# Expert weights in one table per token block, and 24 blocks' outputs for the first token block inside the rounds of inputs

## The reference, cut to what matters

```python
q = (xt @ wq).reshape(PEER_BLOCK, PEER_HEADS, PEER_KEY_DIM)
s1 = jnp.einsum('thd,nd->thn', q[..., :PEER_HALF], subkeys1)
s2 = jnp.einsum('thd,nd->thn', q[..., PEER_HALF:], subkeys2)
v1, i1 = lax.top_k(s1, PEER_TOPK)
v2, i2 = lax.top_k(s2, PEER_TOPK)
cand = (v1[..., :, None] + v2[..., None, :])          # 16 x 16 candidates
vals, pos = lax.top_k(cand, PEER_TOPK)
ids = e1 * PEER_N_KEYS + e2                           # one of 16384 experts
g = jax.nn.softmax(vals, axis=-1)
a = jnp.einsum('td,thkd->thk', xt, u_tab[ids])
hid = jax.nn.gelu(a) * g
y = jnp.einsum('thk,thkd->td', hid, v_tab[ids])
x = layer_norm(DN_ALPHA * x + y, ln2_g, ln2_b)
```

## Time and profile before

| | us |
|---|---|
| three runs, median | 1095.2 |
| lowest and highest | 1092.23, 1096.01 |
| the profiled execution | 1094.1 |
| its span in the trace | 1092.1 |
| PE busy | 1019.6 (93%) |
| DVE busy | 837.4 (77%) |
| POOL busy | 453.3 (42%) |
| ACT busy | 450.8 (41%) |

### The profile page before, as it was taken

How to read it: one execution, slowest core, us unless ns; L and a number is a source line. 1 busy time by engine, 2 the same in 40 slices (tenths; PEclk the granted TensorE clock), 3 DMA queues, 4 the chain that set the end, 5 groups by cost and what they waited for, 6 DMA issues and landing times.

```text
span 1092.1 us, 20382 instructions
## 1 busy us (share of the span) xinstructions
PE 1019.6 (93%) x6766; PEld 935.8 (86%) x6766; DVE 837.4 (77%) x1484; ACT 450.8 (41%) x648; POOL 453.3 (42%) x332
## 2 busy tenths in 40 slices
PE   7999999899999999999999999129999999999995
PEld 6878897899999999999999999128888888888884
DVE  3475457677999998988888888028888888888887
ACT  3474444344443334444444444004444444444442
POOL 5800000058888888888888888840000000000000
PEclk9999999899999999999999999659999999999998
DMA  9676688545665566877777775247777777777773
GB/s 310 233 270 222 208 289 299 177 117 113 140 135 138 146 139 150 199 172 169 159 176 170 173 167 103 0 120 239 238 240 241 241 241 240 240 242 240 243 239 126
DMA packets 146735, 210.41 MB, mean 193 GB/s; under 512 B 47376, under 2 KB 95312, under 8 KB 146704
## 3 DMA queue, kind: packets, MB, share of 16 engines
q1 hardware_dynamic: 109264, 208.58, 58.5%
q0 software_dynamic: 37440, 1.43, 9.9%
HBM read 192.00 MB, written 17.96 MB: 192 GB/s over the span
## 4 chain that ended last, share of the span: by engine, by line
PE 49%; POOL 38%; issue 8%; DVE 3%; ACT 1%; DMA 1%; POOLq 0%; DVEq 0%; SPq 0%; ACTq 0%
POOL expert_weights L457 38%; PE ps L1274 32%; PE ps L1192 14%; PE ps L1088 1%; ACT w_hi L575 1%; DVE w_lo L902 1%; PE ps L1066 1%; DMA xres<-in_x_dram 1%; DVE xres L701 0%; DVE xres L708 0%; PE ps L1038 0%; PE ps L1076 0%; DMA expert_weights<-gw,cell 0%; DVE small L689 0%; DVE v_lo L982 0%
## 5 line engine op out<-in xcount | busy, mean ns | idle before, releaser
L457 POOL DMA_INDIRECT expert_weights<-gw,cell x256 | 413.5, 1615 | 258.9 <-DVE gw L895 178.7
L1232 PE MATMUL ps<-act_hi,uT_hi 128*128 128x256 f32 x1024 | 295.1, 288 | 0.0
L1232 PE MATMUL ps<-act_hi,uT_lo 128*128 128x256 f32 x1024 | 289.9, 283 | 0.0
L1232 PE MATMUL ps<-act_lo,uT_hi 128*128 128x256 f32 x1024 | 289.7, 283 | 0.0
L655 ACT ACTIVATE v_hi<-v_raw 128x512 fp32r<-128x512 f32 x256 | 147.9, 626 | 245.1 <-PE ps L1274 198.3
L1274 PE MATMUL ps<-v_hi,hid_hi 128*128 128x512 f32 x512 | 158.4, 391 | 45.0 <-DVE v_lo L982 45.0
L1232 PEld LDWEIGHTS ps<-act_lo,uT_hi 128*128 128x128 f32 x1024 | 196.6, 192 | 0.0
L1232 PEld LDWEIGHTS ps<-act_hi,uT_hi 128*128 128x128 f32 x1024 | 196.6, 192 | 0.0
L1232 PEld LDWEIGHTS ps<-act_hi,uT_lo 128*128 128x128 f32 x1024 | 196.3, 192 | 0.0
L982 DVE TENSOR_TENSOR v_lo<-v_raw,v_hi 128x512 fp32r<-128x512 f32 x256 | 164.9, 686 | 0.0
L1274 PE MATMUL ps<-v_lo,hid_hi 128*128 128x512 f32 x512 | 158.1, 390 | 0.0
(11 more groups left out here) (149 smaller groups left out, 1392.2 us busy)
## 6 DMA issues: line engine op xcount, KB each, us to landing
v_raw<-in_peer_v_dram SPq DMA_DIRECT2D x128, 512.0 KB, 4.3
u_raw<-in_peer_u_dram SPq DMA_DIRECT2D x68, 512.0 KB
u_raw<-in_peer_u_dram SPq DMA_DIRECT2D x240, 128.0 KB
w_raw<-in_w_in_dram SPq DMA_DIRECT2D x8, 2048.0 KB, 9.3
expert_weights<-zeros SPq DMA_DIRECT2D x16, 1024.0 KB, 12.4
g_in<-expert_weights SPq DMA_DIRECT2D x128, 128.0 KB, 3.1
w_raw<-in_peer_wq_dram SPq DMA_DIRECT2D x4, 2048.0 KB, 10.7
w_raw<-in_w_out_dram SPq DMA_DIRECT2D x2, 2048.0 KB, 9.5
```

Source lines behind the costliest of these rows:

```text
L457: pool.indirect_dma_start(out=table_cells, out_offset=bass.IndirectOffsetOnAxis(ap=cell[:, t, k:k + 1], axis=0), in_=gw[:, t, k:k + 1], in ...
L1232: ins = pe.matmul(ps[:, bank, 0:T], (uT_hi, uT_hi, uT_lo)[part][:, slot, k, :], (act_hi, act_lo, act_hi)[part][:, k, :], start=(k == 0 and ...
```

## The change

There are five parts.

- **Two tables.** `expert_weights` becomes one table for each token block, 16384 experts by 128 tokens. A load of both halves (`load_g`) now takes pieces of 512 bytes from two places, and a load of one half takes 64 KB.
- **A skewed order of the scatters** (`ORDER`). The first token block runs ahead: its heads follow each other with 16 or 8 scatters of the second block between, and its last scatter is number 192 of 256. The last 64 are heads 4 to 7 of the second block, one behind the other. The last routing batch (heads 4 to 8) becomes two.
- **Fills.** For the last 24 expert blocks (104 to 127, whose `H` is made in the first stage) PE computes the outputs of token block 0 within rounds 13 to 18 of the inputs, one fill behind each slot: two matmuls in full f32, `g_fill` (128 x 128) against `v_fill` (128 x 1024). There are two buffers of each. DVE multiplies `H` into `g_fill` (`fill_hidden`, `fill_hid`), SP loads a pair when fill f - 2 is done (`fill_done`); the first two pairs are loaded when `scattered0` is full.
- **Outputs.** The 24 blocks have only their second token half left in the last stage. The first 24 fours have three whole blocks at k = 0 to 2 and one of these halves at k = 3; 8 fours of whole blocks follow.
- DVE waits for all fills (`fill_done`) before the first `hidden`, since `v_fill0` lies where `hid_hi` and `hid_lo` do.

The core of the diff:

```diff
-BATCHES = ((0, 1, 0, 1), (1, 2, 0, 1), (0, 2, 1, 2), (0, 2, 2, 4), (0, 2, 4, 8))
+BATCHES = ((0, 1, 0, 1), (1, 2, 0, 1), (0, 2, 1, 2), (0, 2, 2, 4), (0, 2, 4, 6), (0, 2, 6, 8))
+ORDER = [(0, 0, 0, 16), (1, 0, 0, 16), (0, 1, 0, 16), (1, 1, 0, 8), (0, 2, 0, 16), (1, 1, 8, 16), (0, 3, 0, 16),
...
+         (0, 7, 0, 16), (1, 4, 0, 16), (1, 5, 0, 16), (1, 6, 0, 16), (1, 7, 0, 16)]
...
-    weights = nc.dram_tensor("expert_weights", (NB * P, T), F32)
+    weights = nc.dram_tensor("expert_weights", (TB, NB * P, P), F32)
...
+        def load_fill(f, slot):
+            b = f + FILL_BLOCK
+            sp.dma_start(g_fill[slot], table[0, bass.ds(b * P, P), :]).then_inc(s[f"g_fill_in{slot}"], 16)
+            sp.dma_start(v_fill[slot][:], v_dram[bass.ds(b * P, P), :]).then_inc(s[f"v_fill_in{slot}"], 16)
...
+        def next_round(i, refill):
             sp.wait_ge(s["u_read"], i + (NPRE + 1))
             load_u(GROUP * i + block_of(NPRE + GROUP), 0)
+            for k in range(GROUP):
+                if k:
+                    sp.wait_ge(s["u_turned"], (GROUP - 1) * i + k)
+                    load_u_squares(GROUP * i + block_of(NPRE + GROUP + k), k)
+                if refill:
+                    f = GROUP * i + (k - GROUP * (FILL_ROUND + 1))
+                    sp.wait_ge(s["fill_done"], f + 1)
+                    load_fill(f + 2, k % 2)
+        with sp.Fori(0, FILL_ROUND) as i:
+            next_round(i, False)
+        sp.wait_ge(s["scattered0"], 16 * SLOTS)
+        for f in range(2):
+            load_fill(f, f)
+        next_round(FILL_ROUND, False)
+        with sp.Fori(FILL_ROUND + 1, ROUNDS - 1) as i:
+            next_round(i, True)
+        for f in range(FILLS - GROUP, FILLS - 2):
+            sp.wait_ge(s["fill_done"], f + 1)
+            load_fill(f + 2, f % 2)
...
+        def main_round(i, first_fills, last_fills):
...
             for k in range(1, GROUP):
                 before = 8 * NPRE if k == 1 else 0
+                if k < 3 and first_fills:
+                    fill_hidden(f + (k - 3), (k + 1) % 2, landed)
+                if k == 3 and last_fills:
+                    fill_hidden(f, 0, landed + 16)
                 turn(n + k, k, 16 * NQ * i + (before + 16 * NQ))
...
+        def fill(f, slot, landed, opens):
+            pe.wait_ge(s["fill_hid"], f + 1)
+            pe.wait_ge(s[f"v_fill_in{slot}"], landed)
+            for d in range(2):
+                ins = pe.matmul(ps[:, d, :], g_fill[slot], v_fill[slot][:, d * 512:(d + 1) * 512], start=opens, stop=False, skip_group_check=True)
+            ins.then_inc(s["fill_done"], 1)
...
+        def mixed_four(i, opens):
+            for k in range(BODY):
+                outputs_of(BODY * i + k, k % 2, k == 3, opens and k == 0)
```

More of the change, by code:

```diff
@@ L884, in route @@
             for t in range(t0, t1):
-                ch.step(dve.tensor_scalar(cell[:, t, ks], ids[:, t, ks], float(T), column[:, t:t + 1],
+                ch.step(dve.tensor_scalar(cell[:, t, ks], ids[:, t, ks], float(P), column[:, t:t + 1],
                                           ALU.mult, ALU.add))
@@ L984, in rest_v, with hidden @@
                                   ALU.subtract).then_inc(s["v_lo_done"], 1)
-        def hidden(m, slot, landed, head):
-            cells = g_in[:, slot, :]
+        def hidden(m, b, slot, landed, head, second):
+            c = P if second else 0
+            cells = g_in[:, slot, c:T]
             dve.wait_ge(s[f"g_in{slot}"], landed)
-            dve.tensor_tensor(cells, H[:, bass.ds(m * T, T)], cells, ALU.mult).then_inc(s["hid_m"], 1)
+            dve.tensor_tensor(cells, H[:, bass.ds(b * T + c, T - c)], cells, ALU.mult).then_inc(s["hid_m"], 1)
             dve.wait_ge(s["hid_m"], m + 1)
@@ L1262, in main_four @@
                     transpose_u(16 * i + (8 * NPRE + 32), 0, 6)
-        with pe.Fori(0, ROUNDS - 1) as i:
-            main_four(i, False)
-        main_four(ROUNDS - 1, True)
+                if fills:
+                    fill(GROUP * i + (k - GROUP * FILL_ROUND), k % 2,
+                         32 * i + (16 * (k // 2 + 1) - 32 * FILL_ROUND), opens and k == 0)
+        with pe.Fori(0, FILL_ROUND) as i:
+            main_four(i, False, False)
+        main_four(FILL_ROUND, False, True, True)
+        with pe.Fori(FILL_ROUND + 1, ROUNDS - 1) as i:
+            main_four(i, False, True)
+        main_four(ROUNDS - 1, True, False)
         def expert_outputs(slot, t, opens, closes):
@@ L1277, in expert_outputs, with outputs_of @@
             return ins
-        def outputs_of(n, slot, opens=False):
+        def outputs_of(n, slot, second=False, opens=False):
             pe.wait_ge(s["hid_done"], n + 1)
             pe.wait_ge(s["v_lo_done"], 2 * n + 2)
-            for t in range(TB):
-                ins = expert_outputs(slot, t, opens, False)
+            for t in range(1 if second else 0, TB):
+                ins = expert_outputs(slot, t, opens and t == 1, False)
             ins.then_inc(s["y_done"], 1)
-        for m in range(2):
-            outputs_of(m, m, m == 0)
-        with pe.Fori(0, (NB - 4) // 2) as i:
+        def mixed_four(i, opens):
+            for k in range(BODY):
+                outputs_of(BODY * i + k, k % 2, k == 3, opens and k == 0)
+        mixed_four(0, True)
+        with pe.Fori(1, FILLS) as i:
+            mixed_four(i, False)
+        with pe.Fori(BODY * FILLS // 2, (NB - 2) // 2) as i:
             for k in range(2):
-                outputs_of(2 * i + (2 + k), k)
+                outputs_of(2 * i + k, k)
         for t in range(TB):
```

119 lines of the change are left out of this document (76 added, 43 removed).

## The result

The changed kernel takes 1139.2 us (median of four runs, 1136.53 to 1139.67) against 1094.2 for the kernel before: a ratio of 1.041, with a 95% interval of 1.040 to 1.043. The change costs 45 us. The forecast was 1120 with a range of 1103 to 1143; the direction and the mechanisms were those named, and the forecast was 19 us too low. The profiled execution took 1139.2 with a span of 1137.0.

A forecast was written before the change was run, and what follows sets the result against it. It took a loop of fill load, DVE product, turn and SP issues to bound the inputs. Outputs start 38.5 us later and take 13.3 less: +25.2 on the profiled 1094.1 is 1119.3, forecast 1120 us, range 1103 to 1143.

The forecast's parts named there:

- The scatter: POOL's 256 scatters: first block lands at 603.6; three waits of at least +1.5 us each; end at 730 to 738.
- The price of a fill: Two f32 matmuls of 512 columns on PE in the input rounds: 1.71 us a fill, 41 us for 24.
- the ring: Input rounds with fills: load, product, turn, four U issues, next load wait on each other; 25.9 us a round.
- my four steps: One input round with fills: two load-to-turn links of 7.0 us, 6.4 to V's landing, 5.5 of PE work.
- The end of the inputs: Last input round on PE: 615 plus five rounds of 25.9 us plus 24 gives 768.5.
- The outputs: Last stage on PE: 337.7 us instead of 351.0, with 24 fours of 10.44 us instead of 10.88.
- The wait behind each half block: Outputs: a half block covers 1.36 us, too short for DVE's next v_lo; PE waits 0.92 us in each four.
- Rival 1: Input rounds: the loop of loads, DVE and SP does not bind; inputs end at 733, whole 1087 to 1097; chance 10%.
- rival 2: Inputs and outputs: neither the load loop nor the wait in each four binds; about 1072 us; chance 3%.
- Rival 4: Input rounds: loads land later still on shared DMA engines; 30 us a round and above, 1143 and more; chance 7%.
- Rival 3: Fill rounds: PE's waits bring its clock to half, +15 to +30 us, 1135 to 1150; chance 8%.
- The sums of the range: Inputs' end by load landings: 757 with the short ones, 780 with the medians, 792 with the longest; whole 1103 to 1143.

The follow-up runs named there:

- both removed: Against the changed kernel: next fill's load put ahead of U's issues, and V of the fills loaded for the first two only; 1097.6 us.
- the kernel with 20 fills: Against the 1074.6 us kernel (early fill load; four places for V, hidden values and weights): 20 fills, not 24, begun a round later; 1075.3 us.
- the fastest kernel: Against the changed kernel: fill load ahead of U's issues, four places for v_hi, v_lo, hid_hi, hid_lo and g_in; 1074.6 us, ratio 0.983.

## Why the prediction came out as it did

- **The scatter.** Foreseen: number 192 landed at 603.6, the end at 730 to 738, POOL waiting at three heads. In the trace number 192 is issued at 598.25 and lands 3.06 us later, at 601.3, and the last is issued at 730.52. With its landing of about 3 us that is 733.5, inside the foreseen range. The three waits:

```profile
632.23 1.54 POOL L512 DMA_INDIRECT expert_weights<-gw,cell  x1 [2.15 <-DMA expert_weights<-gw,cell]
...
665.44 1.54 POOL L512 DMA_INDIRECT expert_weights<-gw,cell  x1 [3.32 <-DMA expert_weights<-gw,cell]
...
699.22 1.54 POOL L512 DMA_INDIRECT expert_weights<-gw,cell  x1 [2.73 <-DMA expert_weights<-gw,cell]
```

- **The price of a fill.** I took 1.71 us from the key scores. A fill that does not wait takes 1.72 (767.93 to 769.65 above). One that comes behind a wait takes 1.98, which I had not allowed for: +0.3 on the ring, whose only fill is such a one. PE's own round is 19.6 (both removed) against my 19.3.
- **The ring: right in kind, 3.2 us too short.** Against the measured links my four steps (7.0, 7.0, 6.4, 5.5) miss 0.4, 1.7, 0.8 and 0.3 us. Two kinds of terms were too small. The first is SP: from a turn's end to the start of the load behind four issues I had 2.0 us. In the second link it was 2.9 (650.44 to 653.35, where one issue took 0.95 us and not 0.33) and 2.3 a round later (680.34 to 682.63); in the third, with `g_fill`'s own issue, 3.0 against my 2.4. The second is the landings. For the 64 KB piece of the second link I took 2.6 us, ends 2.0 and 3.1, by the thought that half of the bytes of `g_in` should land sooner; it took 3.35, in the later rounds of the chain 3.42 and 3.50, and once 2.48. In the first link the 4.10 is what I had (4.1), but 4.92 a round later. V took 4.25 for my 4.0. In the round shown the landings make 1.0 of the 3.2 us, a round later 1.9. Why the 64 KB land so late is open: they came sooner with fewer pieces of U, but also with all the pieces and without the loads of V (above). The figures of the Trainium skill ("DMA: Bandwidth & Descriptors", Anatomy of one DMA), 2.0 us and the bytes over 436 GB/s, would be 2.15 us; they are a fit to DMAs that GpSimd issues, and these are SP's. The measurement of 2.48 to 4.92 decides, and the round by the Trainium skill's figures, an estimated 23.5 (redone, with three landings replaced, 23.8), is further off than mine.
- **The end of the inputs.** Five rounds of 3.3 us more are +16.3; the transposes of round 13 end at 613 and not 615, -2.0; behind the last transposes 22.4 us and not 24, -1.6. Together +12.7: 781.2 against 768.5.
- **The outputs.** The wait behind each half block was right in place and cause, not quite in size: the four is 10.70 and not 10.44. The idle time in brackets, 0.84, is not to be held against my 0.92, since records overlap. By starts, the pair at 886.49 would be followed at 886.94 and is at 887.94: 1.00 us for 0.92. The first pair behind the wait then takes 0.59 to the next start and not 0.453, another 0.14, and the pairs after it the last 0.04. That is the 0.26. 24 times 0.26 is 6.2 of the 7.4 us that the outputs are longer than forecast. The two misses, 12.7 and 7.4, are 20.1, and 1119.3 plus 20.1 is the profiled 1139.2 to 0.2.
- **The rivals.** Rival 1 (no ring) and rival 2 (neither ring nor wait) did not come, and yet rival 2 was well priced as a kernel: with both causes removed it takes 1074.6, where rival 2 said 1072. With the load moved it takes 1104.1, 7 over rival 1's 1087 to 1097, which had no waits for V in it; 1097.6 without them. Rival 4 (30 us a round) was nearly met in size, 29.2, but by its cause, the landings, only in part. Rival 3, the clock, came in part:

```profile
606.00:608.00 2.00, 2.00 (x4) 0.68 (x3) 2.00 (x3) 0.94 (x1) 1.70 (x2) 0.50 1.05 268
610.00:780.00 170.00, 135.67 (x773) 105.59 (x773) 73.00 (x74) 36.72 (x54) 95.27 (x59) 0.92 0.67 163
```

These are windows as in the earlier trace rows: the granted clock is 0.50 (1.2 GHz) at the first fill, behind a wait of PE of some 3.5 us, and 0.92 in the mean over the rounds with fills, where it was 1.00 before. It shows on the ring where one of its few pieces of PE falls into such a stretch, in the last round (granted clock 0.71 and 0.76 in the mean):

```profile
751.42 2.73 PE ps L1343 x4
754.15 3.71 PE ps L1316 x24
```

That is 1.6 us more than in the other rounds of the ring (1.98 and 2.88). The rival's 15 to 30 us did not come. As I read it, a PE that idles a fifth of the time spends the slower matmuls mostly in time that it would have waited; the chain, in which 0.8 us at a time appear and not whole rounds, fits that.
- **The sums of the range.** Two did not come out as written. The inputs' end, 615 plus five rounds plus 24, is 760.5, 776.5 and 789 with rounds of 24.3, 27.5 and 30, and not 757, 780 and 792. With these ends the range is 1106 to 1140.5, and the measured 1139.2 lies inside it by little. And the landings of the earlier trace rows put into the four links give 24.5, 26.9 and 30.9 us a round. The 4.5 MB a round of rival 1 are 4.25. The rounds of 29.2 lie above the medians' 26.9, so the measured time fell into the range because its high end took in the longest landings.

## What to carry to other kernels

Before adding a load to an in-order queue, write down what the queue waits for just ahead of it and who, in the end, releases that wait: here one position in SP's loop cost 35 us, and the busy shares hardly show it (PE 92% with it, 94% without). A block that is half as long halves the cover of everything that is prepared behind it, so double-buffered operands want more places before blocks are cut, and all of them at once: with `v` and `hid` widened and `g_in` not, half of the gain stayed away (14 of 29.5 us came). Work that fills an idle engine is worth its idle time only if its own inputs come early: the same fills made the kernel 4% slower or 1.7% faster.

## What the runs showed of the hardware that I had not expected

- The loads of 64 KB were often no sooner there than the median of 3.1 us for 128 KB in the outputs, and their time changed with what else was loaded. In the ring's second link they took 3.35, 3.42, 3.50 and once 2.48 us behind 512 KB of U; 2.25, 2.34, 2.36 and once 3.23 behind 128 KB; and 2.35 to 2.83 behind 512 KB again, with the loads of V left out.
- An indirect DMA of 128 single elements, on which POOL waits, lands in 2.98 us with little else on the DMA engines. Under the load of the fills it took 7.77 us once in the kernel with 20 fills, and in the fastest kernel 6.64 and 7.23 (at 627.63 and 696.08), with a DMA share of 0.82 from 610 to 740. In the changed kernel (share 0.67 from 610 to 780) the three waits of POOL sum to 8.2 us, without fills to 5.8, and in the fastest kernel to 13.4. The last scatter is issued at 722.6 before the change, 726.8 without fills, 730.5 with the fills as changed, and 737.7 in the fastest kernel; so the skewed order costs 4 us alone and 15 there.
- A matmul group behind a wait is slower by 0.26 us for a fill (1.98 for 1.72) and by some 0.18 in the outputs, also where the granted clock is 1.00, as it is in the changed kernel from 665 to 669.
